# The convolved groups of a Mamba-2 encoder's input projection, multiplied with the weights as the stationary operand

## What is computed

```python
zxbcdt = u @ in_proj                                  # 256 x 2048 times 2048 x 10368
z   = zxbcdt[..., :D_INNER]                           # 4096 columns
xbc = zxbcdt[..., D_INNER:D_INNER + D_XBC]            # 4096 + 2 * 1024 columns
dt_raw = zxbcdt[..., D_INNER + D_XBC:]                # 128 columns
xbc = jax.nn.silu(centred_depthwise_conv(xbc, conv_w, conv_b))   # 5 taps over the tokens
...
dt = jax.nn.softplus(dt_raw + dt_bias)
y = y_fwd + y_bwd + xs * d_skip
gy = rms_norm(y * silu(z)) * norm_w
return gy @ out_proj
```

## Time and profile before

| | |
|---|---|
| median of 3 runs | 2187.15 us (2184.22 to 2187.46) |
| the profiled execution | 2187.26 us |
| its span, first to last instruction | 2185.6 us |
| mean granted clock of TensorE | 0.997 |
| TensorE busy | 2156.2 us (99% of the span) |
| VectorE, ScalarE, GpSimd busy | 1428.6, 1118.2, 223.2 us |

### The profile page before, as it was taken

How to read it: one execution, slowest core, us unless ns; L and a number is a source line. 1 busy time by engine, 2 the same in 40 slices (tenths; PEclk the granted TensorE clock), 3 DMA queues, 4 the chain that set the end, 5 groups by cost and what they waited for, 6 DMA issues and landing times.

```text
span 2185.6 us, 30800 instructions
## 1 busy us (share of the span) xinstructions
PE 2156.2 (99%) x10624; PEld 1816.4 (83%) x10624; DVE 1428.6 (65%) x1732; ACT 1118.2 (51%) x1567; POOL 223.2 (10%) x172
## 2 busy tenths in 40 slices
PE   9999999999999999999999999989999999999997
PEld 7888888888888788888888888878888888888886
DVE  7788787687787656557565655686565655555656
ACT  5677576675775634444444443455444443443433
POOL 0213233132220100001000000032000000000001
PEclk9999999999999999999999999999999999999999
DMA  7959989599595574545555645445555645555553
GB/s 260 283 193 240 245 232 248 178 239 278 168 256 206 197 250 173 196 172 201 183 195 189 212 172 199 166 154 205 200 199 186 215 169 198 185 190 194 192 193 115
DMA packets 247122, 443.99 MB, mean 203 GB/s; under 512 B 14080, under 2 KB 49072, under 8 KB 245376
## 3 DMA queue, kind: packets, MB, share of 16 engines
q1 hardware_dynamic: 206768, 397.52, 53.5%
q0 software_dynamic: 35664, 28.66, 7.7%
q10 hardware_dynamic: 4608, 16.78, 2.0%
HBM read 440.68 MB, written 2.23 MB: 203 GB/s over the span
## 4 chain that ended last, share of the span: by engine, by line
PE 91%; DVE 5%; DMA 2%; ACT 2%; issue 1%; SPq 0%; DVEq 0%; ACTq 0%
PE acc L383 14%; PE acc L385 14%; PE acc L384 14%; PE acc L664 9%; PE acc L674 5%; PE tb L664 5%; PE sbk L664 5%; PE sbk L385 3%; PE tb L384 3%; PE sbk L384 3%; PE tb L385 3%; PE sbk L383 3%; PE tb L383 3%; PE sbk L674 2%; PE tb L674 2%; DVE wlo L1194 2%
## 5 line engine op out<-in xcount | busy, mean ns | idle before, releaser
L777 ACT CAST whi<-raw 128x1024 fp32r<-128x1024 f32 x745 | 771.9, 1054 | 678.2 <-DMA raw<-in_w 280.7
L1194 DVE TENSOR_TENSOR wlo<-raw,whi 128x1024 fp32r<-128x1024 f32 x745 | 915.1, 1265 | 212.9 <-ACT whi L777 208.1
L383 PE MATMUL acc<-whi,xT 128*128 128x512 f32 x828 | 332.8, 402 | 13.8 <-DVE wlo L1194 9.1
L385 PE MATMUL acc<-wlo,xT 128*128 128x512 f32 x828 | 323.6, 391 | 0.0
L384 PE MATMUL acc<-whi,xT 128*128 128x512 f32 x828 | 323.2, 390 | 0.0
L383 PE MATMUL acc<-whi,hTl 128*128 128x512 f32 x736 | 291.3, 396 | 0.3 <-DVE hTl L1214 0.3
L384 PE MATMUL acc<-whi,hTh 128*128 128x512 f32 x736 | 286.6, 389 | 0.0
L385 PE MATMUL acc<-wlo,hTh 128*128 128x512 f32 x736 | 286.5, 389 | 0.0
L664 PE MATMUL acc<-xT,whi 128*128 128x512 f32 x896 | 213.3, 390 | 0.0
L383 PEld LDWEIGHTS acc<-whi,xT 128*128 128x128 f32 x828 | 156.0, 188 | 50.6 <-issue 8.3
L664 PEld LDWEIGHTS acc<-xT,whi 128*128 128x128 f32 x896 | 165.6, 188 | 32.6
(11 more groups left out here) (227 smaller groups left out, 2677.2 us busy)
## 6 DMA issues: line engine op xcount, KB each, us to landing
raw<-in_w SPq DMA_DIRECT2D x512, 512.0 KB, 4.7
raw<-in_in_proj SPq DMA_DIRECT2D x161, 512.0 KB, 5.7
raw<-in_out_proj SPq DMA_DIRECT2D x64, 512.0 KB, 7.3
spare<-in_masks ACTq DMA_DIRECT2D x16, 512.0 KB, 7.9
spare<-f_scratch POOLq DMA_DIRECT2D x32, 256.0 KB, 17.0
area_d<-in_masks ACTq DMA_DIRECT2D x8, 512.0 KB, 6.5
area_d<-f_scratch POOLq DMA_DIRECT2D x16, 256.0 KB, 9.2
area_c<-in_masks ACTq DMA_DIRECT2D x8, 512.0 KB, 7.1
```

The lines of the kernel that those rows point to most:

```text
L383: pe.matmul(dst, lhs[1][:, kt, rows(t)], hi, start=first and i == 0, stop=False)
L385: mm = pe.matmul(dst, lhs[0][:, kt, rows(t)], lo, start=False, stop=end)
L777: act.copy(whi[:, s.slot(RING)], raw[:, r]).then_inc(hi_ready, 1)
L1194: dve.tensor_tensor(wlo[:, slot], raw[:, r], whi[:, slot].bitcast(F32), ALU.subtract).then_inc(lo_ready, 1)
```

## The change

The twelve convolved groups are multiplied as the MLP's `up` does it: weights stationary, four banks a group (128 channels each, all 256 tokens, high and low part of the tokens side by side), results channel by channel. The turns are gone. ScalarE copies the low half of each bank to `cv_low`, VectorE adds it to the high half straight into `cvin` and frees the bank. The first and the last of a group's four blocks are worked in two halves, channels 0 and 1 ahead of 2 and 3. The numbers q move on by two for a convolved group. `dt` is multiplied into `tb`.

```diff
+            def channels_of(q, kt, slot, j, ms, part, first, last, done):
+                for m in ms:
+                    bk = bank(q + m // 2)
+                    dst = bk.tiles[m % 2]
+                    if first:
+                        wait(pe, bk.free[m % 2], bk.need)
+                    cs = slice(m * P, (m + 1) * P)
+                    if part == 0:
+                        mm = pe.matmul(dst[:], whi[:, slot, j, cs], xT_both[:, kt].rearrange("p m n -> p (m n)"),
+                                       start=first, stop=False)
+                    else:
+                        mm = pe.matmul(dst[:, 0:T], wlo[:, slot, j, cs], xT[0][:, kt, :], start=False, stop=last)
+                    if last and m in (1, 2):
+                        mm.then_inc(bk.full, 1)
+                    if done and m == CT - 1:
+                        mm.then_inc(w_used, 1)
...
+            def channels(q, s, after=none):
+                for b in range(KT // SUBK // 2):
+                    units = (2 * b, 2 * b + 1)
+                    if b in (0, KT // SUBK // 2 - 1):
+                        channel_units(q, s, units, (0, 1))
+                        channel_units(q, s, units, (2, 3))
+                    else:
+                        channel_units(q, s, units, range(CT))
+                    after(b)
...
-            def turn_pj(q):
-
-                for t in range(TT):
-                    pe.wait_ge(acc_free[q.slot(2)][t], (q.half() + 1).n)
-                for t in range(TT):
-                    for j in range(CT):
-                        mm = pe.transpose(tb[t][:, j * P:(j + 1) * P], pj[:, t, j * P:(j + 1) * P], ident[:])
-                mm.then_inc(cv_tr, 1)
...
-            wide(Pos(Q_BC), Pos(S_BC))
-            wide(Pos(Q_BC + 1), Pos(S_BC + 8), turn_cols, amid={0: (6, lambda: turn_pj(Pos(Q_BC)))})
...
+            channels(Pos(Q_BC), Pos(S_BC))
+            channels(Pos(Q_BC + 2), Pos(S_BC + 8), turn_cols)
...
+            def low_cv(q, s_end, ms):
+                for m in ms:
+                    bk = bank(q + m // 2)
+                    if m < CT - 1:
+                        act.wait_ge(bk.full, bk.filled.n)
+                    else:
+                        act.wait_ge(w_used, s_end.n)
+                    act.copy(cv_low[:, m, :], bk.tiles[m % 2][:, T:2 * T]).then_inc(cv_low_out, 1)
...
                     if n == 2:
-                        if k > 1:
-                            silu_bc(k - 1)
-                        pj_evac(q, s + 8, 0)
+                        silu_bc(k - 1)
                     if n == 3:
                         if k == 2:
                             dt_steps(2)
-                        pj_evac(q, s + 8, 1)
-                        if k == 1:
-                            silu_bc(0)
+                        for h in range(2):
+                            split_hi(s + (12 + h))
+                            low_cv(q, s + 8, (2 * h, 2 * h + 1))
...
+            def fill_cv(k, q, ms):
+                for m in ms:
+                    bk = bank(q + m // 2)
+                    dve.wait_ge(cv_low_out, (k.times(CT) + (m + 1)).n)
+                    dve.tensor_tensor(cvin[:, m, PAD:PAD + T], bk.tiles[m % 2][:, 0:T], cv_low[:, m, :],
+                                      ALU.add).then_inc(bk.free[m % 2], 1)
```

More of the change, by code:

```diff
@@ new lines, in channel_units @@
+            def channel_units(q, s, units, ms):
+                for part, ready in ((0, hi_ready), (1, lo_ready)):
+                    for i in units:
+                        if 0 in ms:
+                            wait(pe, ready, s + (i + 1))
+                        slot = (s + i).slot(RING)
+                        for j in range(SUBK):
+                            kt = SUBK * i + j
+                            channels_of(q, kt, slot, j, ms, part, part == 0 and kt == 0,
+                                        part == 1 and kt == KT - 1, part == 1 and j == SUBK - 1)
@@ L463, in first_group @@
+            def channels(q, s, after=none):
[7 more added lines that the diff above has]
+                    after(b)
             def first_group():
[L465 removed]
+                q, all_m = Pos(Q_B0), range(CT)
@@ L466, in first_group @@
                 pe.wait_ge(xt_half_lo, 1)
+                pe.wait_ge(row0_hi, 1)
+                channels_of(q, 0, 0, 0, all_m, 0, True, False, False)
                 pe.wait_ge(row0_lo, 1)
-                for t in range(TT):
[L469 to L472, removed]
@@ L473, in first_group @@
-                pe.wait_ge(lo_ready, S_B0 + 1)
-                for t in range(TT):
[L475 to L478, removed]
+                channels_of(q, 0, 0, 0, all_m, 1, False, False, False)
@@ L581, in wide_z @@
             def wide_z(q, s, g, before=None):
[L584 to L588, removed]
+                amid = {3: (TURN_BACK, lambda: turn_back(g))}
+                if before is not None:
+                    amid[0] = (6, lambda: turn_gy(before))
+                wide(q, s, lambda k: chain(g, k), amid=amid)
             warm_up(2)
@@ L911, in after @@
                 def after(k):
-                    if k == 2:
-                        wait(act, off_done, g.times(2) + -1)
-                        pj_evac(q, s + 8, 0)
                     if k == 3:
                         split_hi(s + 12)
+                        wait(act, off_done, g.times(2) + -1)
+                        low_cv(q, s + 8, (0, 1))
                         split_hi(s + 13)
@@ L983, in _ @@
                 split_hi(Pos(S_DT + i))
-            for t in range(TT):
-                pj_evac(Pos(Q_B0), Pos(S_B0 + 8), t)
-                split_hi(Pos(S_DT + 4 + 2 * t))
-                split_hi(Pos(S_DT + 5 + 2 * t))
+            for h in range(2):
+                low_cv(Pos(Q_B0), Pos(S_B0 + 8), (2 * h, 2 * h + 1))
+                split_hi(Pos(S_DT + 4 + 2 * h))
+                split_hi(Pos(S_DT + 5 + 2 * h))
             split_hi(Pos(S_DT + 8))
@@ L1262, in convolve @@
                         if tap == 0:
+                            bk = bank(q + j // 2)
+                            dve.wait_ge(bk.free[j % 2], bk.emptied.n)
                             dve.tensor_scalar(cv[:, j, :], src, w, convb[:, bass.ds(ch.n + j, 1)],
@@ L1592, in _ @@
                 split_lo(Pos(S_B0 + 2 * c + 1))
-            for i in range(8):
+            for i in range(4):
                 split_lo(Pos(S_DT + i))
+            for h in range(2):
+                fill_cv(Pos(0), Pos(Q_B0), (2 * h, 2 * h + 1))
+                split_lo(Pos(S_DT + 4 + 2 * h))
+                split_lo(Pos(S_DT + 5 + 2 * h))
             dve.wait_ge(const_in, 16 * 7)
             dve.wait_ge(w_used, S_DT + 2)
-            dve.tensor_scalar(dtv, acc[Q_DT % 2][0][:, 0:T], dtp[:, 0:1], None, ALU.add).then_inc(
-                acc_free[Q_DT % 2][0], 1)
+            dve.tensor_scalar(dtv, tb[0][:, 0:T], dtp[:, 0:1], None, ALU.add).then_inc(dt_out, 1)
             split_lo(Pos(S_DT + 8))
```

160 lines of the change are left out of this document (76 added, 84 removed).

## The result

| | before | after |
|---|---|---|
| median of nine runs each (lowest to highest), us | 2186.45 (2183.98 to 2188.81) | 2191.94 (2190.39 to 2193.56) |
| profiled execution, us; its span, us | 2187.26; 2185.6 | 2192.42; 2190.7 |
| mean granted clock of TensorE | 0.997 | 0.995 |

The ratio is 1.0027, with a 95% interval from 1.0018 to 1.0035: slower by 5 us. The forecast was 2192.7.

What follows compares the result with a forecast made beforehand. TensorE, busy 2156.2 of 2185.6 us, was taken as the bound. Wait 7.2, cold start 1.9, wider groups 5.3, turns -9.7 and z0 0.7 made +5.4 on 2187.26: 2192.7 us, 8-in-10 range 2188.8 to 2196.5.

Steps and rivals of the forecast that it cites:

- The exchange: Each convolved group on TensorE: losing a turn (0.88 us) against wider multiplications (+0.53) gains 0.35 us.
- rival 4: Convolved groups: 256 columns cost half of 0.227 us, so groups stay at 21.76 us; 2187.4 us in all, chance 0.03.
- The wait at C0: Start of C0: TensorE waits for VectorE's adds of B1, queued behind dt, a Silu and a split; +7.2 us.
- the convolution was not held by the turn: B0's convolution on VectorE, ahead of dt: still starts at 43.59 us, since its weight loads are untouched.
- The cold start: After the wait ahead of C0: TensorE's clock starts at its lower level, +1.9 us (bounds 0 and 3.5).
- rival 1: At C0 and z0: the clock holds through the wait and z0 finds its bank free; +2.8, 2190.1 us, chance 0.17.
- The term of 0.7: Start of z0: TensorE waits for xs0's add, behind a split with late weights; +0.7 us (0 to 2).
- eleven turns are gone: Convolved groups after C0 has begun: TensorE saves eleven turns of 0.88 us each, -9.7 us.
- the wider groups: Ten convolved groups after C0 has begun: each grows by 0.53 us from 256-column multiplications, +5.3 us.
- Rival 3: Start of C0: no wait, if the dt chain were over some 8 us sooner; 2181.4 us, chance 0.07.
- VectorE has a third of its time free over the span: Other borders: 48 more adds on VectorE cost nothing where its queue is ahead of TensorE's need.

Runs made afterwards that it cites:

- e_late: Changed kernel with B0 started only after the second piece of xT has been split: 2190.67 us, one run.
- e_warm9: Changed kernel with nine warm-up multiplications added on TensorE between B1 and C0: 2189.56 us, ratio 1.0012 to the kernel before.
- e_c01_taps: e_early_c01 with two of the five taps left out of the convolutions of B1, C0 and C1: 2187.80 us, ratio 1.0007.
- e_early_c01: Changed kernel with copies and adds of B1, C0 and C1 placed earlier, C0's convolution moved into its own group: 2191.94 us, ratio 1.0026.
- e_all4: e_early_c01 with xs0's copies and adds also placed earlier and the scaling of x behind its group's last splits: 2191.26 us, ratio 1.0020.
- e_z3: Changed kernel with ScalarE's copies of the turned xs ahead of the second decay in group z3 alone: 2192.70 us, one run.
- e_copies: Changed kernel with ScalarE's copies of the turned xs ahead of the second decay in every z group: 2198.46 us, ratio 1.0058.
- e_early_c0: Changed kernel with the copies and adds of B1 and C0 placed earlier on ScalarE and VectorE: 2192.74 us, ratio 1.0028.
- e_warm: Changed kernel with 34 warm-up multiplications added on TensorE between B1 and C0: 2210.12 us, ratio 1.0107.

## Why the prediction was right, and where it was not

- **The exchange.** From xs0's turn to z0's took 22.67 us before (110.65 to 133.32); xs0 now takes 22.30: 0.37 us won, 0.35 foretold. The Trainium skill, "TensorE: Matmul & The Clock Gate", Back-to-back issue gap, would make a group 64 x 215.8 + 64 x 109.2 ns = 20.8 us, an estimate from its N/2.4 + 2.5 ns, which the section gives for a multiplication by itself, saying that with weight loads in the stream both set the spacing. The trace says 22.3, and rival 4, which came close to that rule, is out.
- **The wait at C0** is where it was forecast, for the adds forecast, behind the very operations counted. C0 is 5.5 us late instead of 7.2. The step that failed is "the convolution was not held by the turn, so removing the turn does not bring it forward; the loads ahead of it are untouched": the weights landed at 39.77 instead of 41.36, and the chain came 1.6 us sooner with them. The start of B0's convolution, which it took for fixed, scatters by 1.4 us from run to run (e_late), so how much of this the change did is open. B1 itself ended at 58.1 and not at 60.4, which the wait swallowed, as was said.
- **The cold start** cost 7.52 - 4.64 = 2.9 us (the same 24 multiplications take 4.64 in C1), not 1.9, inside the bounds; e_warm9 shows it by itself. Of rival 1 the half that lets the clock hold is out.
- **z0 did not wait.** Its weights landed 3.6 us after VectorE freed their buffer (128.87 to 132.47), not the 5.3 of the earlier trace rows. The term of 0.7 was nothing, which was the other half of rival 1.
- **Not foreseen:** "eleven turns are gone" was counted as 9.7 us, but z3 and z5 gave 1.4 and 0.9 us of it back. I had asked what the change adds ahead of TensorE's banks, and not whether TensorE would then come too soon for the chain inside a z group. D0 came 0.4 us sooner than counted.
- **The sum**, by the traces: 5.5 for C0's start, 2.9 for the cold start, 10 x 0.54 for the wider groups, -9.7 for the turns, 2.3 for z3 and z5, -0.4 for D0, together 6.0 against 5.3 at D3. The rest is in xs1, xs3, xs5 and xs7, which grew by 0.41 us each and not by 0.54 (xs1 from 26.37 to 26.78), and in D0 with xs2, which grew by 0.34; why, stays open. So the mechanism at C0 was foreseen, but that the total was met to within a microsecond is luck: the smaller wait at C0 and the free z0 made up for the dearer cold start and for z3 and z5.
- **Rival 3** (C0 does not wait: 2181.4 us). What it describes was built in four versions, by another order and not by a shorter `dt` chain, and does not pay: with the wait gone at C0 and C1 and below 1 us at xs0 the time stays within a microsecond of the changed kernel's. "VectorE has a third of its time free over the span" was the wrong reading: between 42 and 130 us it was busy for 71.7 of 88 us already before, and in the new form TensorE depends on it at each border. A part of the owed time answers to VectorE's work (9.6 us less of it gave 4.1 in e_c01_taps).
- **What holds the rest** stays open. The traces point to the landing of the weights, for which ScalarE waits 27 to 31 us between 60 and 130 in e_early_c01, e_c01_taps and e_all4 (22.4 in the kernel before). One candidate, argued and not tried: a weight's buffer is loaded again only after its subtraction, so VectorE, transfer and split wait for each other in turn. Another that no run moved is other traffic: in e_all4 from 78 to 95 us the transfers that GpSimd issues (it adds `f_scratch` to the masks) take 67% of the transfer engines' time for 1.42 MB, and those of SyncE (weights and `x`) 57% for 3.41 MB. In the kernel before it is 69% and 56%, but TensorE waits for nothing there.

## What to carry to other kernels

A change that turns a loose hand-over (a pair of banks, a whole group of time) into a tight one should be priced by the engine on the other side over that stretch, not by its share of the span. When a wait is found, move it before believing in its removal: if it turns up at the next border with the same length, the order is not the cause. And an operation taken from the bounding engine pays only where the chain that it meets next is not late already.

## What the runs showed of the hardware

- A wait of the same length is not always followed by the same cold stretch. After 8.2 us of waiting at C0 the 24 multiplications took 7.52 us (changed kernel) and 7.54 (e_z3), after 8.3 in e_copies 6.39, after 9.0 at xs0 in e_early_c0 6.43, and after 5.0 in e_late 6.55, against 4.64 warm: a loss of 2.9 or of 1.8 to 1.9 us. From 70 to 72 us the granted clock is 0.50 in the changed kernel and 0.97 in e_copies.
- A multiplication of plain fp32 operands with 512 columns takes 0.85 us ((86.92 - 58.14) / 34) and shows as two records; in the fp32r form of the kernel's groups it takes 0.227. In e_warm, 34 of them, up to 86.92:

```profile
58.14 29.35 PE L462 MATMUL sbk<-scores 128*128 128x512 f32 x68
86.92 2.41 PE L473 MATMUL acc<-xT,whi 128*128 128x512 f32 x8
```

- The same VectorE product, 128x512 in z3, took 0.69 us in the changed kernel and 1.41 in e_z3; that is as much as e_z3's new wait. ScalarE's decays ran beside it in both, GpSimd's products only in e_z3. In the changed kernel, VectorE and GpSimd:

```profile
337.64 0.69 DVE L1315 TENSOR_TENSOR area_d<-area_d,scores 128x512 f32<-128x512 f32 x1
339.81 3.16 POOL L1760 TENSOR_TENSOR area_b<-area_b,cols 128x512 f32<-128x512 f32 x2 [14.47 <-ACT area_b L903]
```

In e_z3:

```profile
338.54 1.41 DVE L1319 TENSOR_TENSOR area_d<-area_d,scores 128x512 f32<-128x512 f32 x1
338.36 2.49 POOL L1764 TENSOR_TENSOR area_b<-area_b,cols 128x512 f32<-128x512 f32 x2 [12.12 <-ACT area_b L905]
```

In this stretch of both traces the VectorE operations that begin while GpSimd's products run are the long ones: two subtractions took 4.04 us in e_z3, where they begin at 339.87, and 2.35 in the changed kernel, where they begin at 338.25. It seems that the earlier place of the copies loses a part of what it wins because it lets GpSimd start sooner. No run moved GpSimd's products by themselves, so that they are the cause is argued from the times and not shown by an experiment.
